# A deeper ring of split weight pieces in the expert loop of a hybrid Mamba/GLA/MoE layer

## The chip, the cores and the metric

The kernel runs on one core of one Trainium2 chip, as one program. The metric is the device time of one execution in microseconds. Three runs of the kernel before gave 2230.03, 2230.74 and 2231.86 us; the median, 2230.74 us, is the time that the changed kernel is held against.

## The reference, cut to what matters

The reference is one layer: modulation, two token mixers, and a mixture of experts of which each token takes two out of 32. The change lies in the experts. Tokens are sorted by expert into blocks of 128, and each block goes through one expert's three matrices (1024 x 512, 1024 x 512 and 512 x 1024, float32):

```python
def moe(t, w_router, router_bias, w_gate, w_up, w_down):
    ...
    def expert_block(args):
        xb, e = args
        return (jax.nn.silu(xb @ w_gate[e]) * (xb @ w_up[e])) @ w_down[e]

    yb = lax.map(expert_block, (buf.reshape(n_blocks, MOE_BLOCK, D), block_e))
    y = yb.reshape(-1, D)[dest] * gates.reshape(-1)[order][:, None].astype(t.dtype)
    return jnp.zeros_like(t).at[tok].add(y)
```

## The kernel before

The program is written engine by engine, in stages: modulation and input projection, scans, mixer and output projection, `slots` (which sorts tokens into blocks and writes a plan), `experts`, and `combine` (the final norm). Nothing reorders the instructions; each engine runs its list as written, and semaphores join the lists.

**One block.** `experts` runs a loop body once for each block; bodies come in pairs (`u` = 0 and 1, the helper `pairs`), and 50 bodies do work here. I call them even (u = 0) and odd. TensorE keeps float32 accuracy by splitting each operand into a high part of type fp32r and the rest, and making three products: high x high, low x high, high x low. A weight matrix is cut into two halves of 128 x 2048, called pieces here. The six pieces of a block are numbered by `s`. TensorE's body uses, in this order: s = 2 and 3 (w_up into `pu`), s = 4 (first half of w_gate of the next block, into `pg`), four transposes of `h` into `ph`, s = 5 (second half of that w_gate), eight transposes of the gathered tokens of the block after next into `tx`, then s = 6 and 7 (w_down into `pd`). A piece is 12 matmuls of 512 columns; each piece ends with an increment of the semaphore `used`.

**The split.** ScalarE makes the high part of a piece (`high`, L2456, a copy that rounds), VectorE the low part (`low`, L2575, raw minus high). Both write into rings, `w_hi` and `w_lo`, of three pieces each: piece s stands in slot s % 3, and `high` of piece s waits until piece s - 3 has been used. The two engines work ahead of TensorE: in a body they split s = 5 to 10, and 8 to 10 are the pieces 2 to 4 of the next body. Between the pieces they have other work. ScalarE: `h_hi` (from `ph`), `hs` = SiLU of `pg`, and `x_hi` (from `tx`, two halves). VectorE: `h` = `pu` * `hs`, `h_lo`, `x_lo` (two halves), and `yb` = `pd` * gate (two halves), which starts the block's way out. GpSimd then adds `yb` to the rows of `x_mid` by an indirect DMA, and gathers tokens by another.

**Registers.** Which expert and which of its two raw buffers a piece comes from stands in a table, the plan. Each engine loads entries of it into registers (`entry`); ScalarE loads six at the start of a body, VectorE three. The raw weights come by DMAs that SyncE issues, 2 MB for each matrix, as soon as the low part of the last piece in the other raw buffer is made.

Of the kernel before, what the change touches and what calls it, by code (L numbers as in the profile page):

```python
# [18 lines left out]
ACT = mybir.ActivationFunctionType  # L19
F32 = mybir.dt.float32  # L20
# [3 lines left out]
P = 128  # L24
# [95 lines left out]
def build(nc, A, out, debug=()):  # L120
# [16 lines left out]
    with ExitStack() as top:  # L137
# [60 lines left out]
        if "stop2" in debug:  # L198
            return
        early.close()  # L200
        route = {
            "logits": keep("logits", [P, LT, NE]), "gate": keep("gate", [P, LT, 2]),
            "bias": keep("bias", [P, NE]), "down_g": keep("down_g", [P, NG]), "down_e": keep("down_e", [P, NE]),
        }
        route["hot"] = [route["logits"], keep("hot1", [P, LT, NE])]
        mixer(nc, A, C, K, route, tok_rec, feat_rec, back_state, fwd_chunk, qk_rec, a_rows, zg_rec, w_gated, x_mid, h_rows)
# [4 lines left out]
        with ExitStack() as ctx:  # L211

            weights = [ctx.enter_context(nc.sbuf_tensor(n, [P, 2, KT * FF], F32)) for n in ("w_gates", "w_ups", "w_downs")]
            names = Names(nc, ctx, "wts")
            loaded = [names(f"{n}_loaded") for n in ("gates", "ups", "downs")]
            toks = ctx.enter_context(nc.sbuf_tensor("toks", [P, TAB, 2], I32))
            route["plan"] = ctx.enter_context(nc.sbuf_tensor("plan", [1, PL_LEN], I32))
            gate_bc = ctx.enter_context(nc.sbuf_tensor("gate_bc", [P, D], F32))
            seat(nc, ctx, "we", 96)
            w_hi = ctx.enter_context(nc.sbuf_tensor("w_hi_e", [P, 3, PIECE], mybir.dt.float32r))  # L220
            slots(nc, A, C, route, toks, weights, loaded, gate_bc, w_hi, x_mid, h_rows)
            experts(nc, A, C, route, toks, weights, loaded, gate_bc, w_hi, h_rows, x_mid)
        combine(nc, A, x_mid, out)
# [1810 lines left out]
EARLY_T = LT - 2  # L2034
PIECE = KT // 2 * FF


# [289 lines left out]

def experts(nc, A, C, route, toks, parts, w_loaded, gate_bc, w_hi, h_rows, x_mid):

    mod, ident, plan = C["mod"], C["ident"], route["plan"]
# [3 lines left out]
    with ExitStack() as ctx:  # L2342
# [14 lines left out]
        hs, h = sb("hs", [P, FF]), sb("h", [P, FF])  # L2357
        h_hi, h_lo = sb("h_hi", [P, KF, P], F32R), sb("h_lo", [P, KF, P], F32R)
        yb = sb("yb", [P, D])
        to = [sb(f"to{b}", [P, 2], I32) for b in range(2)]  # L2360
# [83 lines left out]
        SPLITS = {5: (0, 1, 1), 6: (2, 0, 0), 7: (2, 1, 0), 8: (1, 0, 1), 9: (1, 1, 1), 10: (0, 0, 2)}  # L2444

        def raw(part, half, place):
            return parts[part][:, place, PIECE * half:PIECE * (half + 1)]

        @block.scalar
        def _(act):  # L2450

            act.wait_ge(credited, 1)

            def high(s, part, half, place):

                act.activation(w_hi[:, s % 3:s % 3 + 1, :], raw(part, half, place), ACT.Copy).then_inc(hi_done, 1)  # L2456

# [8 lines left out]
            for s, part, half in ((2, 1, 0), (3, 1, 1)):  # L2466
                act.wait_ge(w_loaded[part], 16)
                if s == 3:
                    act.wait_ge(used, 1)
                high(s, part, half, slice(0, 1))  # L2470
                if s == 2:
                    features(1, 1)
# [4 lines left out]
            hold(act, w_loaded[0], order * 16 + 16, act_held)  # L2477
            high(4, 0, 0, bass.ds(par, 1))

            def body(r, u):  # L2480
                b = r * 2 + u
                pars = [entry(act, b + n, PL_PAR, 1) for n in range(3)]
                orders = [entry(act, b + n, PL_ORDER, NE - 1) for n in range(3)]

                def piece(s):
                    part, half, n = SPLITS[s]
                    if half == 0:

                        hold(act, w_loaded[part], orders[n] * 16 + 16, act_held)

# [12 lines left out]
                features(b + 2, u)  # L2503
                piece(9)
                piece(10)
# [4 lines left out]
        def _(pe):  # L2510
# [9 lines left out]

            def product(s, b, acc, a_hi, a_lo, k, at, start, stop):

                c = slice(at, at + 512)
                for n, (a, w) in enumerate(((a_hi, w_hi), (a_lo, w_hi), (a_hi, w_lo))):
                    mm = pe.matmul(acc[:, :], a[:, k, :], w[:, s % 3, c], start=start and n == 0, stop=stop and n == 2)  # L2525
                return mm

            def wide(b, s, half, u, acc):

                pe.wait_ge(lo_done, b * 6 + (s + 1 + CREDIT))  # L2530
                for k in range(4):
                    mm = product(s, b, acc, x_hi[u], x_lo[u], 4 * half + k, FF * k, half + k == 0, half == 1 and k == 3)
                mm.then_inc(used, 1)

            turn(0, 0, 0)
            pe.wait_ge(xlo_done, 2)
            wide(0, 0, 0, 0, pg)
            turn(1, 0, 1)
            wide(0, 1, 1, 0, pg)

            def body(r, u):
                b = r * 2 + u
                wide(b, 2, 0, u, pu)
                wide(b, 3, 1, u, pu)

                pe.wait_ge(xlo_done, b * 2 + 4)
                pe.wait_ge(silu_done, b + 1)
                wide(b, 4, 0, 1 - u, pg)
# [4 lines left out]
                wide(b, 5, 1, 1 - u, pg)  # L2553
                turn(b + 2, r + 1, u)
                pe.wait_ge(hlo_done, b + 1)

                pe.wait_ge(y_copied, b * 2 + 2)
                for half in range(2):
                    s = 6 + half
                    pe.wait_ge(lo_done, b * 6 + (s + 1 + CREDIT))  # L2560
                    for k in range(2):
                        for n in range(2):
                            mm = product(s, b, pd[n], h_hi, h_lo, 2 * half + k, D * k + 512 * n, half + k == 0, half + k == 2)
                    mm.then_inc(used, 1)
# [3 lines left out]
        def _(dve):  # L2568
# [3 lines left out]

            def low(s, part, half, place):

                dve.tensor_tensor(w_lo[:, s % 3:s % 3 + 1, :], raw(part, half, place), w_hi[:, s % 3:s % 3 + 1, :].bitcast(F32),  # L2575
                                  ALU.subtract).then_inc(lo_done, 1)
# [7 lines left out]
            for s, part, half in ((0, 0, 0), (1, 0, 1), (2, 1, 0), (3, 1, 1)):  # L2584
                dve.wait_ge(hi_done, s + 1)
                low(s, part, half, slice(0, 1))
                if s == 0:
# [4 lines left out]
            dve.wait_ge(hi_done, 5)  # L2592
            low(4, 0, 0, bass.ds(par, 1))

            def body(r, u):
                b = r * 2 + u
                pars = [entry(dve, b + n, PL_PAR, 1) for n in range(3)]

                def piece(s):
                    part, half, n = SPLITS[s]  # L2600
                    dve.wait_ge(hi_done, b * 6 + (s + 1))
                    low(s, part, half, bass.ds(pars[n], 1))
# [109 lines left out]
```

## Time and profile before

| what | us |
|---|---|
| median of three runs (2230.03 to 2231.86) | 2230.74 |
| the profiled execution, its own time | 2230.2 |
| its span, from the first to the last record | 2228.4 |
| busy in the span: TensorE, VectorE, ScalarE, GpSimd | 2056.6, 1662.9, 1184.4, 515.5 |

The expert loop fills about 920 us of the span, from 1237 to 2159 us; ahead of it stand the other stages, behind it a tail of 70 us that ends the last block's output and runs `combine`. A busy share is no measure of how full TensorE is, since matmuls overlap each other in the record (one is shown with 0.39 us, the next starts 0.23 us later); the distance between the starts of the same matmul in two bodies tells what a body costs. In a timeline a bracket behind a row tells how long the engine was idle ahead of it and what ended that.

### The profile page before, as it was taken

How to read it: one execution, taken by the hardware profiler on the slowest of the kernel's cores; microseconds unless marked ns; L12 is line 12 of the kernel's file. 1: busy time of each engine (PE TensorE's matmuls, PEld its weight loads, DVE VectorE, ACT ScalarE, POOL GpSimd, SP SyncE). 2: the span in 40 equal slices, each digit the busy share in tenths (PEclk: the TensorE clock that was granted, in tenths of full speed). 3: DMA queues.
4: the chain of work that ended last, by engine and by line, in shares of the span. 5: the costliest groups of instructions: out<-in, count | busy, mean ns of one | idle time of the engine just before them, and what ended most of it. 6: DMA issues, size and time to landing. Idle time of an engine off the chain costs nothing. (4 is left out here: it accounts for less than half of the span.)

```text
span 2228.4 us, 38461 instructions
## 1 busy us (share of the span) xinstructions
PE 2056.6 (92%) x12690; PEld 1701.4 (76%) x12690; DVE 1662.9 (75%) x2132; ACT 1184.4 (53%) x1564; POOL 515.5 (23%) x537
## 2 busy tenths in 40 slices
PE   5999999989999979999984999999999999999970
PEld 3998888877777768888873788888888888888850
DVE  3555555556766667777756899999999999999973
ACT  3433333434555523434332677777777777777753
POOL 1000000000100123323221233333333333333332
PEclk8999999999999969999996999999999999999995
DMA  9443344356988599999937374789888599799957
GB/s 303 157 137 126 126 142 160 109 209 203 334 293 305 209 307 338 296 325 304 302 98 266 97 242 104 234 282 304 262 282 285 168 315 365 244 356 303 376 140 311
DMA packets 219973, 541.34 MB, mean 243 GB/s; under 512 B 15968, under 2 KB 56923, under 8 KB 213339
## 3 DMA queue, kind: packets, MB, share of 16 engines
q1 hardware_dynamic: 186856, 428.68, 53.9%
q0 software_dynamic: 30512, 102.77, 17.9%
q10 hardware_dynamic: 2499, 8.45, 0.9%
q8 instruction: 69, 1.13, 0.2%
q14 instruction: 37, 0.30, 0.0%
HBM read 404.26 MB, written 135.59 MB: 242 GB/s over the span
## 5 line engine op out<-in xcount | busy, mean ns | idle before, releaser
L2456 ACT ACTIVATE w_hi_e<-w_gates 128x2048 fp32r x101 | 194.0, 1920 | 149.6 <-issue 102.7
L2575 DVE TENSOR_TENSOR w_lo_e<-w_gates,w_hi_e 128x2048 fp32r<-128x2048 f32 x103 | 236.5, 2297 | 31.2 <-ACT w_hi_e L2456 29.8
L2575 DVE TENSOR_TENSOR w_lo_e<-w_ups,w_hi_e 128x2048 fp32r<-128x2048 f32 x102 | 233.3, 2287 | 35.3 <-ACT w_hi_e L2456 35.3
L723 PE MATMUL pf<-x_hi,wide 128*128 128x256 f32 x1152 | 244.7, 289 | 11.1 <-DVE x_lo L850 11.1
L2575 DVE TENSOR_TENSOR w_lo_e<-w_downs,w_hi_e 128x2048 fp32r<-128x2048 f32 x100 | 228.1, 2281 | 0.0
L2456 ACT ACTIVATE w_hi_e<-w_ups 128x2048 fp32r (+1 forms) x102 | 195.4, 1915 | 21.7 <-PE pd_e L2525 21.7
L723 PE MATMUL pf<-x_lo,wide 128*128 128x256 f32 x720 | 204.7, 284 | 0.0
L723 PEld LDWEIGHTS pf<-x_hi,wide 128*128 128x128 f32 x1152 | 192.3, 194 | 16.2 <-issue 15.9
L2456 ACT ACTIVATE w_hi_e<-w_downs 128x2048 fp32r x100 | 191.0, 1910 | 0.5
L2525 PE MATMUL pg_e<-w_hi_e,x_hi_e 128*128 128x512 f32 x408 | 167.2, 410 | 9.6 <-DVE w_lo_e L2575 8.1
L2434 POOL DMA_INDIRECT x_mid<-yb_e,to_e x50 | 127.5, 2551 | 190.1 <-DVE yb_e L2620 188.0
L2525 PE MATMUL pd_e<-w_hi_e,h_hi_e 128*128 128x512 f32 x400 | 161.9, 405 | 0.0
L2525 PE MATMUL pg_e<-w_lo_e,x_hi_e 128*128 128x512 f32 x408 | 161.4, 396 | 0.0
L2525 PE MATMUL pg_e<-w_hi_e,x_lo_e 128*128 128x512 f32 x408 | 160.9, 394 | 0.0
L2525 PE MATMUL pu_e<-w_lo_e,x_hi_e 128*128 128x512 f32 x400 | 158.2, 395 | 0.0
L2525 PE MATMUL pu_e<-w_hi_e,x_lo_e 128*128 128x512 f32 x400 | 157.9, 395 | 0.0
L2525 PE MATMUL pd_e<-w_hi_e,h_lo_e 128*128 128x512 f32 x400 | 157.7, 394 | 0.0
L2525 PE MATMUL pu_e<-w_hi_e,x_hi_e 128*128 128x512 f32 x400 | 157.7, 394 | 0.0
L2525 PE MATMUL pd_e<-w_lo_e,h_hi_e 128*128 128x512 f32 x400 | 157.6, 394 | 0.0
L2413 POOL COPY idx_e<-toks 128x1 int32 (+1 forms) x54 | 56.7, 1050 | 417.0 <-DMA x_mid<-yb_e,to_e 338.9
L723 PEld LDWEIGHTS pf<-x_lo,wide 128*128 128x128 f32 x720 | 139.1, 193 | 0.0
L2415 POOL DMA_INDIRECT xg_e<-h_rows,idx_e x54 | 104.0, 1925 | 43.1 <-POOL idx_e L2413 42.3
(475 smaller groups left out, 4824.9 us busy)
## 6 DMA issues: line engine op xcount, KB each, us to landing
w_gates<-in_w_gate_dram SPq DMA_DIRECT2D x32, 2048.0 KB, 11.5
w_ups<-in_w_up_dram SPq DMA_DIRECT2D x32, 2048.0 KB
w_downs<-in_w_down_dram SPq DMA_DIRECT2D x32, 2048.0 KB, 10.2
recs<-tok_rec SPq DMA_DIRECT2D x17, 968.0 KB, 8.0
qk<-in_w_mod_dram SPq DMA_DIRECT2D x16, 1024.0 KB, 6.7
abc_m<-a_rows SPq DMA_DIRECT2D x16, 1024.0 KB, 7.1
qk_rec<-qk SPq DMA_DIRECT2D x14, 1024.0 KB, 3.9
qk<-qk_rec SPq DMA_DIRECT2D x14, 1024.0 KB, 8.1
```

The source lines that it names most:

```text
L723: mm = pe.matmul(pf[n % 2][:, f % 2, :], a[f][:, k, :], b[:, k, :], start=(k == 0 and j == 0), stop=(k == KT - 1 and j == 2))
L2413: pool.tensor_copy(idx[u][:, :], toks[:, bass.ds(b, 1), 0]).then_inc(idx_ready, 1)
L2415: pool.indirect_dma_start(out=xg[u][:, :], out_offset=None, in_=h_rows, in_offset=bass.IndirectOffsetOnAxis(ap=idx[u][:, 0:1], axis=0)).th ...
L2434: pool.indirect_dma_start(out=x_mid, out_offset=bass.IndirectOffsetOnAxis(ap=to[u][:, 0:1], axis=0), in_=yb[:, :], in_offset=None, compute ...
L2456: act.activation(w_hi[:, s % 3:s % 3 + 1, :], raw(part, half, place), ACT.Copy).then_inc(hi_done, 1)
L2525: mm = pe.matmul(acc[:, :], a[:, k, :], w[:, s % 3, c], start=start and n == 0, stop=stop and n == 2)
L2575: dve.tensor_tensor(w_lo[:, s % 3:s % 3 + 1, :], raw(part, half, place), w_hi[:, s % 3:s % 3 + 1, :].bitcast(F32), ALU.subtract).then_inc( ...
```

## The change

Both rings get four slots: piece s of body u stands in slot (6u + s) % 4, and `high` of piece s waits until piece s - 4 has been used. The room comes from two tiles that are dropped: `hs` now lies in the memory of the masks `incl` and `incl_bd` (joined in one tile `incls`), and `yb` in that of the router's `logits` and `hot1` (joined in `choice`); the experts read neither. In a body ScalarE now makes pieces 5, 6 and 7 ahead of `h_hi` (before: 5 and 6), and piece 8 behind it, ahead of SiLU (before: 7 there, and 8 behind SiLU). VectorE makes piece 5 ahead of `h` (before: behind it), then 6 and 7, and then `h_lo` (before: 5 and 6 between `h` and `h_lo`). Both engines load a register right ahead of the first piece that needs it, and no longer all at the body's start; the number of loads in a body stays the same. TensorE's order is unchanged.

```diff
-        C["incl"], C["incl_bd"] = keep("incl", [P, 2, P]), keep("incl_bd", [P, 2, P])
+        incls = keep("incls", [P, 2, 2, P])
...
+RING = 4
...
-        w_lo = sb("w_lo", [P, 3, PIECE], F32R)
+        w_lo = sb("w_lo", [P, RING, PIECE], F32R)
...
+        def slot(u, s):
+
+            return (6 * u + s) % RING
...
             def body(r, u):
                 b = r * 2 + u
-                pars = [entry(act, b + n, PL_PAR, 1) for n in range(3)]
-                orders = [entry(act, b + n, PL_ORDER, NE - 1) for n in range(3)]
+                pars = {}
 
                 def piece(s):
                     part, half, n = SPLITS[s]
+                    if n not in pars:
+                        pars[n] = entry(act, b + n, PL_PAR, 1)
                     if half == 0:
-
-                        hold(act, w_loaded[part], orders[n] * 16 + 16, act_held)
-
-                    hold(act, used, b * 6 + (s - 2), act_held)
-                    high(s, part, half, bass.ds(pars[n], 1))
+                        hold(act, w_loaded[part], entry(act, b + n, PL_ORDER, NE - 1) * 16 + 16, act_held)
+
+                    hold(act, used, b * 6 + (s - 3), act_held)
+                    high(u, s, part, half, bass.ds(pars[n], 1))
                 piece(5)
                 piece(6)
+                piece(7)
                 act.wait_ge(ht_ps, b + 1)
                 act.activation(h_hi[:, :, :], ph[:, :].rearrange("p (k c) -> p k c", k=KF), ACT.Copy).then_inc(hhi_done, 1)
-                piece(7)
+                piece(8)
 
                 act.wait_ge(used, b * 6 + 6)
                 act.wait_ge(h_done, b + 1)
                 act.activation(hs[:, :], pg[:, :], ACT.Silu).then_inc(silu_done, 1)
-                piece(8)
                 features(b + 2, u)
                 piece(9)
                 piece(10)
...
+                piece(5)
                 dve.wait_ge(used, b * 6 + 4)
                 dve.wait_ge(silu_done, b + 1)
                 dve.tensor_tensor(h[:, :], pu[:, :], hs[:, :], ALU.mult).then_inc(h_done, 1)
-                piece(5)
                 piece(6)
+                piece(7)
                 dve.wait_ge(hhi_done, b + 1)
                 dve.tensor_tensor(h_lo[:, :, :], ph[:, :].rearrange("p (k c) -> p k c", k=KF), h_hi[:, :, :].bitcast(F32),
                                   ALU.subtract).then_inc(hlo_done, 1)
-                piece(7)
                 piece(8)
```

How the two lists stand now. On ScalarE, from the last piece of an even body (s = 10, w_gates) into the odd body, before; a TENSOR_LOAD is a register load, of which six stand in the first gap:

```order
L2456 ACTIVATE w_hi_e<-w_gates 128x2048
L2376 TENSOR_LOAD plan
...
L2456 ACTIVATE w_hi_e<-w_gates 128x2048
...
L2456 ACTIVATE w_hi_e<-w_downs 128x2048
L2496 ACTIVATE h_hi_e<-ph_e 128x512
...
L2456 ACTIVATE w_hi_e<-w_downs 128x2048
...
L2501 ACTIVATE hs_e<-pg_e 128x512
...
L2456 ACTIVATE w_hi_e<-w_ups 128x2048
```

The same stretch of ScalarE's list after the change:

```order
L2455 ACTIVATE w_hi_e<-w_gates 128x2048
L2371 TENSOR_LOAD plan
...
L2455 ACTIVATE w_hi_e<-w_gates 128x2048
...
L2455 ACTIVATE w_hi_e<-w_downs 128x2048
...
L2455 ACTIVATE w_hi_e<-w_downs 128x2048
L2494 ACTIVATE h_hi_e<-ph_e 128x512
...
L2455 ACTIVATE w_hi_e<-w_ups 128x2048
...
L2499 ACTIVATE incls<-pg_e 128x512
```

One load stands between piece 10 and piece 5 in place of six; two moved ahead of piece 6, one ahead of piece 8 and two ahead of piece 10. Piece 7 (the second w_downs) passed `h_hi`, and piece 8 (w_ups) passed SiLU.

On VectorE, from piece 10 of the even body over `yb` into the odd body, before:

```order
L2575 TENSOR_TENSOR w_lo_e<-w_gates,w_hi_e 128x2048
L2620 SCALAR_TENSOR_TENSOR yb_e<-pd_e,to_e,gate_bc 128x512 x2
L2376 TENSOR_LOAD plan
...
L2605 TENSOR_TENSOR h_e<-pu_e,hs_e 128x512
...
L2575 TENSOR_TENSOR w_lo_e<-w_gates,w_hi_e 128x2048
...
L2575 TENSOR_TENSOR w_lo_e<-w_downs,w_hi_e 128x2048
L2609 TENSOR_TENSOR h_lo_e<-ph_e,h_hi_e 128x512
...
L2575 TENSOR_TENSOR w_lo_e<-w_downs,w_hi_e 128x2048
```

The same stretch of VectorE's list after the change:

```order
L2572 TENSOR_TENSOR w_lo_e<-w_gates,w_hi_e 128x2048
L2619 SCALAR_TENSOR_TENSOR choice<-pd_e,to_e,gate_bc 128x512 x2
L2371 TENSOR_LOAD plan
...
L2572 TENSOR_TENSOR w_lo_e<-w_gates,w_hi_e 128x2048
...
L2605 TENSOR_TENSOR h_e<-pu_e,incls 128x512
L2371 TENSOR_LOAD plan
...
L2572 TENSOR_TENSOR w_lo_e<-w_downs,w_hi_e 128x2048
...
L2572 TENSOR_TENSOR w_lo_e<-w_downs,w_hi_e 128x2048
L2609 TENSOR_TENSOR h_lo_e<-ph_e,h_hi_e 128x512
```

Piece 5 (w_gates) passed `h`, piece 7 (the second w_downs) passed `h_lo`; two pieces stand between `h` and `h_lo` as before, but they are 6 and 7.

## Rows read from the trace of the kernel before

**Rows 1.** Busy time by engine in one stretch of the expert loop, with columns
```profile
core 0: us, PE busy (x) PEld busy (x) DVE busy (x) ACT busy (x) POOL busy (x), PEclk, DMA share, GB/s
1700.00:1800.00 100.00, 99.19 (x457) 80.30 (x456) 93.25 (x67) 72.25 (x54) 35.54 (x22) 1.00 0.71 226
```
**Rows 2.** Timeline of TensorE, odd body from 1514.68, even from 1532.92: start, duration
```profile
1514.68 0.39 PE L2525 MATMUL pu_e<-w_hi_e,x_hi_e 128*128 128x512 f32 x1
...
1520.27 0.40 PE L2525 MATMUL pg_e<-w_hi_e,x_hi_e 128*128 128x512 f32 x1
...
1523.05 0.60 PE L2551 MATMUL ph_e<-ident,h_e 128*128 128x128 f32 x4
1523.57 0.50 PE L2525 MATMUL pg_e<-w_hi_e,x_hi_e 128*128 128x512 f32 x1
...
1526.47 1.03 PE L2518 MATMUL tx_e<-ident,xg_e 128*128 128x128 f32 x8
1527.26 0.48 PE L2525 MATMUL pd_e<-w_hi_e,h_hi_e 128*128 128x512 f32 x1
...
1532.92 0.39 PE L2525 MATMUL pu_e<-w_hi_e,x_hi_e 128*128 128x512 f32 x1
...
1542.15 0.50 PE L2525 MATMUL pg_e<-w_hi_e,x_hi_e 128*128 128x512 f32 x1 [0.27 <-DVE w_lo_e L2575]
...
1551.49 0.39 PE L2525 MATMUL pu_e<-w_hi_e,x_hi_e 128*128 128x512 f32 x1
```
**Rows 3.** Waits from 1100 to 2200 us: in total, times, longest
```profile
PE pg_e L2525 <- DVE w_lo_e L2575: 8.1, 26, 1.3
```
**Rows 4.** Timeline of ScalarE, the same two bodies
```profile
1518.69 1.92 ACT L2456 ACTIVATE w_hi_e<-w_gates 128x2048 fp32r x1 [1.72 <-issue]
...
1528.97 1.08 ACT L2461 ACTIVATE x_hi_e<-tx_e 128x512 fp32r<-128x512 f32 x2
1530.48 1.92 ACT L2456 ACTIVATE w_hi_e<-w_ups 128x2048 fp32r x1 [0.43 <-PE pd_e L2525]
1533.28 1.92 ACT L2456 ACTIVATE w_hi_e<-w_gates 128x2048 fp32r x1 [0.88 <-PE pd_e L2525]
1537.69 1.92 ACT L2456 ACTIVATE w_hi_e<-w_gates 128x2048 fp32r x1 [2.49 <-issue]
```
**Rows 5.** Timeline of VectorE, the same two bodies
```profile
1519.32 1.40 DVE L2620 SCALAR_TENSOR_TENSOR yb_e<-pd_e,to_e,gate_bc 128x512 f32<-128x512 f32 x2
1520.64 0.68 DVE L2605 TENSOR_TENSOR h_e<-pu_e,hs_e 128x512 f32<-128x512 f32 x1
1521.24 2.28 DVE L2575 TENSOR_TENSOR w_lo_e<-w_gates,w_hi_e 128x2048 fp32r<-128x2048 f32 x1
...
1525.64 0.68 DVE L2609 TENSOR_TENSOR h_lo_e<-ph_e,h_hi_e 128x512 fp32r<-128x512 f32 x1
...
1529.21 2.29 DVE L2575 TENSOR_TENSOR w_lo_e<-w_ups,w_hi_e 128x2048 fp32r<-128x2048 f32 x1 [0.69 <-ACT w_hi_e L2456]
1531.42 1.28 DVE L2581 TENSOR_TENSOR x_lo_e<-tx_e,x_hi_e 128x512 fp32r<-128x512 f32 x2
...
1535.34 2.29 DVE L2575 TENSOR_TENSOR w_lo_e<-w_gates,w_hi_e 128x2048 fp32r<-128x2048 f32 x1 [0.44 <-ACT w_hi_e L2456]
...
1539.77 2.33 DVE L2575 TENSOR_TENSOR w_lo_e<-w_gates,w_hi_e 128x2048 fp32r<-128x2048 f32 x1 [0.22 <-ACT w_hi_e L2456]
```
**Rows 6.** Timelines of TensorE, VectorE and SyncE at the loop's end
```profile
2158.31 0.40 PE L2525 MATMUL pd_e<-w_lo_e,h_hi_e 128*128 128x512 f32 x1
...
2163.17 1.40 DVE L2620 SCALAR_TENSOR_TENSOR yb_e<-pd_e,to_e,gate_bc 128x512 f32<-128x512 f32 x2
...
2181.92 0.84 SPq L2650 DMA_DIRECT2D x_c<-x_mid  x2
```
**Rows 7.** Timeline of ScalarE near 2104 us
```profile
2103.87 1.92 ACT L2456 ACTIVATE w_hi_e<-w_gates 128x2048 fp32r x1 [0.88 <-PE pd_e L2525]
```
**Rows 8.** The w_gates transfer issued at 2084.45 us, in the densest stretch of loads
```profile
DMA to landing us min/median/max: 16.1/16.1/16.1
```

More of the change, by code:

```diff
@@ L201, in build @@
         route = {
-            "logits": keep("logits", [P, LT, NE]), "gate": keep("gate", [P, LT, 2]),
+            "gate": keep("gate", [P, LT, 2]),
             "bias": keep("bias", [P, NE]), "down_g": keep("down_g", [P, NG]), "down_e": keep("down_e", [P, NE]),
         }
-        route["hot"] = [route["logits"], keep("hot1", [P, LT, NE])]
+        choice = keep("choice", [P, 2, LT, NE])
+        route["hot"] = [choice[:, n] for n in range(2)]
+        route["logits"] = route["hot"][0]
         mixer(nc, A, C, K, route, tok_rec, feat_rec, back_state, fwd_chunk, qk_rec, a_rows, zg_rec, w_gated, x_mid, h_rows)
@@ L2452, in _, with high @@
             act.wait_ge(credited, 1)
-            def high(s, part, half, place):
-                act.activation(w_hi[:, s % 3:s % 3 + 1, :], raw(part, half, place), ACT.Copy).then_inc(hi_done, 1)
+            def high(u, s, part, half, place):
+                n = slot(u, s)
+                act.activation(w_hi[:, n:n + 1, :], raw(part, half, place), ACT.Copy).then_inc(hi_done, 1)
             def features(b, u):
@@ L2467, in _ @@
                 act.wait_ge(w_loaded[part], 16)
-                if s == 3:
-                    act.wait_ge(used, 1)
-                high(s, part, half, slice(0, 1))
+                high(0, s, part, half, slice(0, 1))
                 if s == 2:
@@ L2519, in turn, with product, wide @@
                     mm.then_inc(xt_ps, 1)
-            def product(s, b, acc, a_hi, a_lo, k, at, start, stop):
+            def product(s, u, acc, a_hi, a_lo, k, at, start, stop):
                 c = slice(at, at + 512)
                 for n, (a, w) in enumerate(((a_hi, w_hi), (a_lo, w_hi), (a_hi, w_lo))):
-                    mm = pe.matmul(acc[:, :], a[:, k, :], w[:, s % 3, c], start=start and n == 0, stop=stop and n == 2)
+                    mm = pe.matmul(acc[:, :], a[:, k, :], w[:, slot(u, s), c], start=start and n == 0, stop=stop and n == 2)
                 return mm
-            def wide(b, s, half, u, acc):
+            def wide(b, v, s, half, u, acc):
                 pe.wait_ge(lo_done, b * 6 + (s + 1 + CREDIT))
                 for k in range(4):
-                    mm = product(s, b, acc, x_hi[u], x_lo[u], 4 * half + k, FF * k, half + k == 0, half == 1 and k == 3)
+                    mm = product(s, v, acc, x_hi[u], x_lo[u], 4 * half + k, FF * k, half + k == 0, half == 1 and k == 3)
                 mm.then_inc(used, 1)
@@ L2562, in body @@
                         for n in range(2):
-                            mm = product(s, b, pd[n], h_hi, h_lo, 2 * half + k, D * k + 512 * n, half + k == 0, half + k == 2)
+                            mm = product(s, u, pd[n], h_hi, h_lo, 2 * half + k, D * k + 512 * n, half + k == 0, half + k == 2)
                     mm.then_inc(used, 1)
@@ L2571, in _, with low @@
             dve.sem_inc(credited, 1)
-            def low(s, part, half, place):
-                dve.tensor_tensor(w_lo[:, s % 3:s % 3 + 1, :], raw(part, half, place), w_hi[:, s % 3:s % 3 + 1, :].bitcast(F32),
+            def low(u, s, part, half, place):
+                n = slot(u, s)
+                dve.tensor_tensor(w_lo[:, n:n + 1, :], raw(part, half, place), w_hi[:, n:n + 1, :].bitcast(F32),
                                   ALU.subtract).then_inc(lo_done, 1)
@@ L2585, in _ @@
                 dve.wait_ge(hi_done, s + 1)
-                low(s, part, half, slice(0, 1))
+                low(0, s, part, half, slice(0, 1))
                 if s == 0:
@@ L2592, in _ @@
             dve.wait_ge(hi_done, 5)
-            low(4, 0, 0, bass.ds(par, 1))
+            low(0, 4, 0, 0, bass.ds(par, 1))
             def body(r, u):
                 b = r * 2 + u
-                pars = [entry(dve, b + n, PL_PAR, 1) for n in range(3)]
+                pars = {}
                 def piece(s):
                     part, half, n = SPLITS[s]
+                    if n not in pars:
+                        pars[n] = entry(dve, b + n, PL_PAR, 1)
                     dve.wait_ge(hi_done, b * 6 + (s + 1))
-                    low(s, part, half, bass.ds(pars[n], 1))
+                    low(u, s, part, half, bass.ds(pars[n], 1))
+                piece(5)
                 dve.wait_ge(used, b * 6 + 4)
```

25 lines of the change are left out of this document (13 added, 12 removed).

## The prediction

> **What bounds the kernel now.** I read the busy time by stretches first. In the expert loop TensorE shows 99.19 us in 100, at a granted clock of 1.00, VectorE 93.25 and ScalarE 72.25 [rows 1]. So two engines are nearly full, and a share of busy time can't say which one sets the pace. The timeline of TensorE can: an odd body lasts from 1514.68 to 1532.92, 18.24 us, and the even one behind it to 1551.49, 18.57 us [rows 2]. In the odd body no row has a bracket: TensorE goes from product to product, and 18.24 us is what its list costs. The even body has one bracket, 0.27 us at the first product of piece 5, which waited for VectorE's low part. With the drain of the transposes ahead of it that makes 18.57 - 18.24 = 0.33 us. The group of waits has 26 such stalls and 8.1 us [rows 3]: two belong to the first body (the longest, 1.3 us, is there), and 24 are those of the even bodies 2 to 48. TensorE is the bound, and it loses 24 x 0.33 us and a start.
>
> Why is piece 5 late in even bodies alone? VectorE starts its low part 0.22 us after it could, waiting for ScalarE's high part [rows 5]. ScalarE starts that high part after 2.49 us in which it waited for nothing but its own instructions (in the odd body 1.72 us) [rows 4]: the six register loads, in the even body with the loop's branch as well. They follow high part 10, which itself waited for its slot (0.88 us, released by the last products of `pd` [rows 4]). So two things make the chain late: a ring of three, and six loads in one place. The change takes away both.
>
> The last thing I read is the end. TensorE's last product starts at 2158.31, so a next body would start 0.23 us later, at 2158.54; yet `yb` of this block starts only at 2163.17 [rows 6], 4.63 us behind. All through the loop VectorE runs that far behind TensorE: in the odd body `yb` starts at 1519.32, 4.64 us after the body's start [rows 2, 5]. Inside the loop nobody waits for `yb`; at the end everything does.
>
> **The change part by part.** It removes no work from TensorE, VectorE or ScalarE: the same pieces, the same six and three register loads. Whether TensorE still waits is worked out by laying the new lists along a body of 18.24 us, whose start is 0. From the odd body [rows 2]: piece 4 starts at 5.59, the transposes of `h` at 8.37, piece 5 at 8.89, the transposes of `tx` at 11.79, piece 6 at 12.58; piece 7, half of `pd` later, at 15.41. ScalarE starts 0.36 us after a slot is given back (1533.28 against 1532.92 [rows 2, 4]), VectorE 0.14 us after a high part ends (1533.28 + 1.92 to 1535.34 [rows 4, 5]).
>
> ScalarE first. High part 5 may start when the piece four earlier has been used, the last one of the body before: 0.36. High 6: 2.80 + 0.36 = 3.16. High 7: 5.59 + 0.36 = 5.95, done at 7.9. `h_hi` follows the transposes, 9.0 to 9.6; high 8 from 9.6 to 11.5; SiLU at 12.0; the two `x_hi` to 13.6; high 9 from there to 15.5; high 10 when piece 6 has been used, 15.41 + 0.36 = 15.77, to 17.7.
>
> VectorE: low 10 starts at 17.83 and takes 2.20 (two low parts fit in 1521.24 to 1525.64 [rows 5]), so `yb` starts at 20.03, that is 1.8 in the next body, and ends at 3.1. Low 5, whose high part has long been ready, runs to 5.3. `h` needs both pieces of `pu`: 5.59 + 0.36 = 5.95, so it ends at 6.6, and the transposes want it at 8.37: 1.7 to spare. Low 6 and low 7 run to 10.95, `h_lo` to 11.6, wanted at 12.58: 0.9 to spare. Before, `h` and `h_lo` started at the same places, 5.96 and 10.96 (1520.64 and 1525.64 less 1514.68 [rows 2, 5]), with two low parts between them, and TensorE didn't wait; so this deadline is no tighter than it was. Low 5 ends at 5.3 and is wanted at 8.89. Low 8 from 11.65, `x_lo` to 15.1, low 9 from 15.6, low 10 at 17.83: the cycle closes. Summed, VectorE has 6 x 2.20 + 1.32 + 0.60 + 0.60 + 1.28 = 17.0 us of work in 18.24, and it now idles where it waits for TensorE.
>
> The terms. (1) The 24 even bodies drop from 18.57 to 18.24: 24 x 0.33 = 8 us. Its bounds are 0 and that. (2) The tail: `yb` starts 1.8 instead of 4.63 us behind TensorE's end, 2.8 us less, once; at best it starts right behind the last product, 2158.31 + 0.40 + 0.36, which gives 4.1, and at worst nothing. What lies between `yb` and the first load of `combine` at 2181.92 [rows 6] hangs on `yb` and moves with it. (3) The first body: here the rings are still empty, both lists start late, and its stalls are shortened, but low 7 now stands ahead of `h_lo` when VectorE is behind. I take 0.6, between 0 and 1.7 (8.1 less 24 x 0.27 [rows 2, 3]). (4) The loads of registers in new places: 1.72 us idle and the 1.92 us of the high part ahead of it for six loads [rows 4] is at most 0.61 us each. One ahead of high 5 and two ahead of high 6 fit between those starts (0.36, 3.16 and the high part of 1.92). The two ahead of high 10 cost nothing if they run under high 9, and 2 x 1.72 / 6 = 0.57 us behind its end if they don't, when high 10 starts at 16.06 in place of 15.77. I take nothing, since on VectorE three loads stand between `yb` and `h`, and 1519.32 + 1.32 = 1520.64 leaves no gap [rows 2, 5]; the bound is 0.3 of term 2. The Trainium skill's page Perfetto Trace Analysis, section Sequencer Loop, says that a sequencer pushes engine instructions into a queue and executes control instructions itself; by that the loads run under the activation ahead of them. VectorE's rows agree; ScalarE's idle 1.72 us fits both readings. By that rule term 2 is 2.8, without it 2.5. (5) `hs` and `yb` at other addresses: no row shows the two at theirs and others, so I take nothing; TensorE has 1.7 us to spare behind `h`, and `yb` isn't waited for in the loop, which bounds it at some tenths either way in the tail.
>
> (6) The transfers. Every low part ends some 3 us earlier in a body (low 7 at 10.95 against 1528.52 less 1514.68 = 13.84, `h_lo` from 1525.64, then 0.60 and 2.28 [rows 5]), and the loads that wait for it start that much earlier; high 10, the first to read a new expert's w_gates, comes 18.6 - 15.8 = 2.8 us earlier (1533.28 - 1514.68 = 18.6 [rows 2, 4]). In the densest stretch a w_gates transfer takes 16.1 us [rows 8] to land, so it is there at 2100.55; the high part 10 that reads it starts at 2103.87 [rows 7], released by TensorE and not by the transfer. So 3.3 us were left, and about as many are left now. If one lands late, TensorE has low 10 in hand until 5.59 of the body after, 3.8 us later than it is made. I cost it at nothing.
>
> Sum: 2230.2 - 8.0 - 2.8 - 0.6 = 2218.8 us for the profiled execution. That one lies 0.5 us under the median of the runs, so the median should come to **2219.3 us**.
>
> **The rivals.** *A, the tail stays.* The end hangs on something other than `yb`, on GpSimd's queue or the last gather. For it: GpSimd does the output's DMA in its own order. Against it: in the timeline it waits for `yb`. Time: 2219.3 + 2.8 = 2222.1. *B, the change doesn't do what it says.* The stall only moves, to `h_lo` at piece 6 (0.9 us to spare, the least) or to a transfer in dense stretches; even bodies stay near 18.57. For it: VectorE is at 93%. Against it: the deadlines above. Time: 2230.7 less the tail, 2228 to 2231. *C, slower: `h` is now behind low 5.* Before, `h` needed no piece; now it stands in VectorE's list behind low 5, and that behind high 5. If high 5 starts where it started (4.77 in the even body: 1537.69 - 1532.92; 4.01 in the odd one: 1518.69 - 1514.68 [rows 2, 4]), low 5 runs from 6.83 to 9.03 and from 6.07 to 8.27, `h` ends at 9.7 and 8.95, and the transposes, wanted at 8.37, stall 1.4 and 0.6 us: 25 x (1.4 - 0.33 + 0.6) = 42 us, 2272 in all. It decides from the point where high 5 starts later than 8.37 - 0.68 - 2.20 - 0.14 - 1.92 = 3.4 us into a body. For it: five of the six loads only moved. Against it: none of them stands ahead of high 5 but one, and high 10 ends at 17.7, so even a whole load and the branch behind it, 0.61 + 0.77, end near 0.9.
>
> **How the numbers follow.** Forecast 0.76 (2217 to 2221.5), A 0.09, B 0.09, C 0.06. About 0.2%, 4.5 us, is what a measurement of this kernel can tell from no change, so faster means under 2226.3: the forecast and A, 0.85; the same: B, 0.09; slower: C, 0.06. The range takes in the forecast and A: from 2216, where tail and first body give all that they can, to 2224, where A has half of the even stalls left. B and C are outside.
>
> **What would show it.** Starts of the first `pu` product all 18.24 us apart from the second body on, and no bracket on `pg` from VectorE: term 1. `yb` about 1.8 us behind the body's start, in the loop and at its end: term 2. High 5 starting near 0.4, and no idle time on ScalarE that waits for nothing: term 4. A bracket at the transposes of `h` means C, one at the first `pd` product means B. I am wrong if even bodies still last 18.5 us, or if all 50 grow.

## The result and the profile after

The changed kernel takes 2210.07 us (median of four runs, 2207.72 to 2212.87), the kernel before beside it 2230.39 us (2226.56 to 2231.86): a ratio of 0.9906, 95% interval 0.9895 to 0.9918. That is 20.3 us less. The forecast was 11.4 us less, 2219.3, and the time lies below the range, which began at 2216. The direction was right, the size was not. Run again later on another occasion, the kernel took 2209.55 us, ratio 0.9905 (0.989 to 0.992).

The profiled execution took 2212.35 us, with a span of 2210.6. It answers to 2230.2 and 2228.4 of before, 17.9 us less; its expert loop started 2.9 us later (1239.63 against 1236.75 us), behind stages that the change leaves alone, and with that added back the difference is 20.7 us, within half a microsecond of that of the medians.

The same stretch of the loop as in [rows 1], busy time by engine:

```profile
core 0: us, PE busy (x) PEld busy (x) DVE busy (x) ACT busy (x) POOL busy (x), PEclk, DMA share, GB/s
1700.00:1800.00 100.00, 100.00 (x470) 82.07 (x469) 94.91 (x67) 74.93 (x57) 37.91 (x23) 1.00 0.71 223
```

TensorE's record now has no idle time at all in this stretch, and it starts 470 instructions in 100 us where it started 457: 2.8% more, although its busy time rose by 0.8% only. (The stretch is no whole number of bodies; by the body lengths below the gain in pace is 2.1%.) The timeline of TensorE, an odd body from 1511.86 and the even one from 1529.89, answers to [rows 2]:

```profile
1511.86 0.39 PE L2522 MATMUL pu_e<-w_hi_e,x_hi_e 128*128 128x512 f32 x1
...
1520.23 0.60 PE L2548 MATMUL ph_e<-ident,h_e 128*128 128x128 f32 x4
1520.58 0.48 PE L2522 MATMUL pg_e<-w_hi_e,x_hi_e 128*128 128x512 f32 x1
...
1523.44 1.03 PE L2515 MATMUL tx_e<-ident,xg_e 128*128 128x128 f32 x8
...
1529.89 0.39 PE L2522 MATMUL pu_e<-w_hi_e,x_hi_e 128*128 128x512 f32 x1
...
1547.92 0.39 PE L2522 MATMUL pu_e<-w_hi_e,x_hi_e 128*128 128x512 f32 x1
```

Both bodies last 18.03 us. Before, they lasted 18.24 and 18.57. Even bodies lost the stall that was forecast, and odd bodies, which were to be the floor, lost 0.2 us as well. The place is the four transposes of `h`: from their start to the start of piece 5 it was 1523.57 - 1523.05 = 0.52 us in the odd body before [rows 2], and is 1520.58 - 1520.23 = 0.35 us now; piece 5 behind them lasted 2.90 us up to the first transpose of `tx` and lasts 2.86. VectorE in the same odd body, answering to [rows 5]:

```profile
1513.71 1.40 DVE L2619 SCALAR_TENSOR_TENSOR choice<-pd_e,to_e,gate_bc 128x512 f32<-128x512 f32 x2
1515.03 2.28 DVE L2572 TENSOR_TENSOR w_lo_e<-w_gates,w_hi_e 128x2048 fp32r<-128x2048 f32 x1
1517.65 0.69 DVE L2605 TENSOR_TENSOR h_e<-pu_e,incls 128x512 f32<-128x512 f32 x1 [0.34 <-PE pu_e L2522]
1518.48 4.49 DVE L2572 TENSOR_TENSOR w_lo_e<-w_downs,w_hi_e 128x2048 fp32r<-128x2048 f32 x2
1522.89 0.68 DVE L2609 TENSOR_TENSOR h_lo_e<-ph_e,h_hi_e 128x512 fp32r<-128x512 f32 x1
```

Low 5 is done 3.3 us ahead of its use, `h` waits for `pu`, and `yb` starts 1.85 us into the body where it started 4.64 us in. That is not the same in every body: over the 50 it is 1.84 to 2.72 us, where it was 4.63 or 4.64 before. ScalarE, answering to [rows 4]:

```profile
1512.24 1.92 ACT L2455 ACTIVATE w_hi_e<-w_gates 128x2048 fp32r x1 [0.88 <-PE pd_e L2522]
...
1520.86 0.60 ACT L2494 ACTIVATE h_hi_e<-ph_e 128x512 fp32r<-128x512 f32 x1 [1.13 <-PE ph_e L2548]
1522.40 1.92 ACT L2455 ACTIVATE w_hi_e<-w_ups 128x2048 fp32r x1 [0.94 <-issue]
```

High 5 starts 0.38 us into the body (before: 4.0 and 4.8). The register load now stands ahead of high 8, and there ScalarE idles 0.94 us (0.40 to 1.28 us over the 50 bodies). The loop's end, timelines of TensorE, VectorE and SyncE, answering to [rows 6]:

```profile
2142.57 0.40 PE L2522 MATMUL pd_e<-w_lo_e,h_hi_e 128*128 128x512 f32 x1
...
2145.47 1.40 DVE L2619 SCALAR_TENSOR_TENSOR choice<-pd_e,to_e,gate_bc 128x512 f32<-128x512 f32 x2
...
2164.16 0.84 SPq L2649 DMA_DIRECT2D x_c<-x_mid  x2
```

`yb` starts 2145.47 - 2142.80 = 2.67 us behind TensorE's end instead of 4.63, and `combine` starts 18.69 us behind it, as before (18.75).

### The profile page after: what moved, and what is told of

Read it like the earlier page. It is cut to its first block and busy times, and to the rows that moved or that the text cites. A ratio compares the mean times of both kernels' runs of the same rounds, so it can differ in the third digit from the quotient of the medians.

```text
span 2210.6 us, 38485 instructions
## 1 busy us (share of the span) xinstructions
PE 2047.3 (93%) x12690; PEld 1702.9 (77%) x12690; DVE 1663.9 (75%) x2132; ACT 1185.3 (54%) x1564; POOL 538.0 (24%) x537
## 5 line engine op out<-in xcount | busy, mean ns | idle before, releaser
L2429 POOL DMA_INDIRECT x_mid<-choice,to_e x50 | 140.6, 2812 | 134.7 <-DVE choice L2619 132.6
```

Of the source, the lines that this page charges most:

```text
L2429: pool.indirect_dma_start(out=x_mid, out_offset=bass.IndirectOffsetOnAxis(ap=to[u][:, 0:1], axis=0), in_=yb[:, :], in_offset=None, compute ...
```

## The experiments

Two theories stood against each other for the 0.2 us that every body lost beyond the forecast. **H, a hidden wait:** in the kernel before TensorE waited for low part 5 in odd bodies too, without a bracket. **L, the layout** or something else that moved: the transposes or the operations on `hs` and `yb` became faster. A second question was which of the three edits (ring, order of the pieces on the two engines, place of the register loads) carries the gain. The table has what the traces gave; bodies are the distances between the first `pu` products, as means over 24 even and 25 odd bodies, the lag is from TensorE's end to the last `yb`.

| kernel | first body | even | odd | lag | ratio to before (95%) |
|---|---|---|---|---|---|
| before | 20.30 | 18.57 | 18.23 | 4.63 | 1 |
| changed | 19.83 | 18.03 | 18.03 | 2.67 | 0.9906 (0.9895 to 0.9918) |
| layout alone | 20.31 | 18.57 | 18.24 | 4.64 | 1.0 (0.9991 to 1.001) |
| ring alone | 20.29 | 18.19 | 18.07 | 4.09 | 0.9933 (0.9916 to 0.9949) |
| order alone (piece 5 ahead of `h`) | 21.28 | 19.57 | 18.77 | 4.64 | 1.0192 (1.0173 to 1.021) |
| loads alone | 18.74 | 18.69 | 18.51 | 5.38 | 1.0047 (1.0029 to 1.0066) |
| loads and piece 5 ahead of `h` | 18.77 | 18.64 | 18.63 | 4.63 | 1.0038 (1.0023 to 1.0053) |
| ring and piece 5 ahead of `h` | 22.84 | 18.15 | 18.10 | 4.10 | 0.9936 (0.992 to 0.9953) |
| changed, `h` first again | 18.73 | 18.50 | 18.32 | 3.33 | 0.9989 (0.9979 to 0.9998) |
| changed, loads at the start again | 22.84 | 18.03 | 18.03 | 1.84 | 0.9916 (0.9903 to 0.993) |
| changed, `yb` ahead of piece 10 | 19.83 | 18.30 | 18.09 | 0.21 | 0.9938 (0.9918 to 0.9958) |
| the same, VectorE's loads at the start | 20.98 | 18.03 | 18.03 | 0.20 | 0.9908 (0.9893 to 0.9923) |

**Layout alone.** The kernel before with `hs` and `yb` at their new addresses:

```diff
-        hs, h = sb("hs", [P, FF]), sb("h", [P, FF])
+        h = sb("h", [P, FF])
...
-        yb = sb("yb", [P, D])
...
+            hs, yb = incls[:, :, :, :].rearrange("p a b c -> p (a b c)"), choice[:, :, :, :].rearrange("p a b c -> p (a b c)")
```

> The kernel before with one thing changed: hs lies in the memory of the masks and yb in that of the router's tiles, ring of three, old orders. Theory H: nothing moves, bodies of 18.57 and 18.23 us, 2230 within 3 us. Rival L: the transposes of h or the operations on hs and yb are faster at the new addresses, both bodies lose 0.2 us, about 2220.

Measured 2232.66 against 2231.63 us: no difference, and no body moved by more than 0.04 us. L has lost its first form, the new addresses.

**`h` first again.** The changed kernel with VectorE's old order:

```diff
-                piece(5)
                 dve.wait_ge(used, b * 6 + 4)
                 dve.wait_ge(silu_done, b + 1)
                 dve.tensor_tensor(h[:, :], pu[:, :], hs[:, :], ALU.mult).then_inc(h_done, 1)
+                piece(5)
                 piece(6)
-                piece(7)
...
+                piece(7)
                 piece(8)
```

> The changed kernel with one thing put back: VectorE makes h ahead of piece 5 again (and h_lo between pieces 6 and 7). Theory H (hidden wait): in the kernel before TensorE waited for low part 5 in every body, also where the trace shows no bracket, and its own list costs 18.03 us. Then h runs from 5.95 to 6.55 us of a body, low 5 ends at 8.83, TensorE wants it at 8.72, so each body lasts 18.2 to 18.25 us, the transposes of h are followed by piece 5 after about 0.52 us and not 0.35, and the time is 49 x 0.2 = 10 us above the changed kernel, about 2220. Rival L (layout): the 0.2 us came from the new addresses of hs and yb or from something else that is kept here; then bodies stay at 18.03 us and the time at 2210.

Measured 2229.06 against 2231.63 us. H expected 2220, L 2210. Bodies went back to 18.32 and 18.50 us with all else kept, so L's second form falls too, and the order on VectorE is needed, as H says; but they overshot what H expected. VectorE and TensorE show both the wait and the overshoot; VectorE first, then TensorE:

```profile
1501.15 0.69 DVE L2604 TENSOR_TENSOR h_e<-pu_e,incls 128x512 f32<-128x512 f32 x1 [1.12 <-PE pu_e L2522]
1502.09 2.29 DVE L2572 TENSOR_TENSOR w_lo_e<-w_gates,w_hi_e 128x2048 fp32r<-128x2048 f32 x1 [0.25 <-issue]
...
1520.42 2.29 DVE L2572 TENSOR_TENSOR w_lo_e<-w_gates,w_hi_e 128x2048 fp32r<-128x2048 f32 x1 [0.17 <-issue]
```
```profile
1504.44 0.51 PE L2522 MATMUL pg_e<-w_hi_e,x_hi_e 128*128 128x512 f32 x1 [0.19 <-DVE w_lo_e L2572]
...
1522.77 0.50 PE L2522 MATMUL pg_e<-w_hi_e,x_hi_e 128*128 128x512 f32 x1
```

Piece 5 starts at 1504.44, 0.06 us behind low 5's end (1502.09 + 2.29 = 1504.38), and in the odd body at 1522.77, again 0.06 us behind it (1522.71). One of the two has a bracket and the other has none; both wait. That is the sign, and the rows of before had it already: in the even body 1542.15 against 1539.77 + 2.33 = 1542.10, in the odd one 1523.57 against 1521.24 + 2.28 = 1523.52 [rows 2, 5], 0.05 us in each. The overshoot is the register load that now stands between `h` and low 5: 0.25 and 0.17 us in which VectorE waits for nothing but its own list. Without these the bodies would last about 18.25 and 18.15 us (an estimate: 18.50 and 18.32 less the two), so the old order by itself costs 0.1 to 0.2 us a body here and the load the rest.

The wait does have a bracket in the kernel before, on other rows. The profile lists TensorE's weight loads (PEld) apart from its products. In the odd body of [rows 2] the one that follows the four of the transposes waited for low 5:

```profile
1522.82 0.59 PEld L2551 LDWEIGHTS ph_e<-ident,h_e 128*128 128x128 f32 x4
1523.57 0.19 PEld L2525 LDWEIGHTS pg_e<-w_hi_e,x_hi_e 128*128 128x128 f32 x1 [0.16 <-DVE w_lo_e L2575]
```

In the view of waits from 1100 to 2200 us that [rows 3] is taken from, the weight loads have a row of their own. It counts one stall at piece 5 in each of the 50 bodies and one more in the first. Before, and then the changed kernel, where only that one more is left:

```profile
PEld pg_e L2525 <- DVE w_lo_e L2575: 18.6, 51, 1.5
```
```profile
PEld pg_e L2522 <- DVE w_lo_e L2572: 0.9, 1, 0.9
```

**Ring alone.** The kernel before with four slots and the room for them:

```diff
-                    hold(act, used, b * 6 + (s - 2), act_held)
+                    hold(act, used, b * 6 + (s - 3), act_held)
```

> The kernel before with the ring of four (and the layout that makes room for it), register loads all at the body's start and old orders. Theory H: high 10 starts 2 us earlier or more, six loads behind it take 3.6 to 4.4 us from its start, so high 5 starts 1 to 2 us into a body and not 4 to 4.8; low 5 then follows h directly, 5.95 + 0.60 + 2.28 = 8.83, and TensorE wants it at 8.72: all bodies 18.2 to 18.25 us, the bracket of the even bodies gone, 24 x 0.33 = 8 us and about 1 us of tail, about 2221. If the ring alone made the whole gain: 18.03 us, 2210. If the loads made the even body late and not the ring: 18.57 and 18.23, 2230.

Measured 2218.04 against 2231.63 us, ratio 0.9933: two thirds of the gain. The bodies are shorter than expected, 18.07 and 18.19 us (the even ones 18.16 without the last, which lasted 18.91 because a high part waited 1.8 us for its w_gates transfer). VectorE lags less, 4.1 us instead of 4.6, so `h` starts as soon as `pu` is there, 5.85 us into the even body shown where it started 5.96 us in, and low 5 with it. The wait is nearly gone, not wholly; VectorE, then TensorE:

```profile
1500.62 0.69 DVE L2606 TENSOR_TENSOR h_e<-pu_e,incls 128x512 f32<-128x512 f32 x1 [0.35 <-PE pu_e L2526]
1501.23 2.28 DVE L2576 TENSOR_TENSOR w_lo_e<-w_gates,w_hi_e 128x2048 fp32r<-128x2048 f32 x1
```
```profile
1503.13 0.60 PE L2552 MATMUL ph_e<-ident,h_e 128*128 128x128 f32 x4
1503.57 0.50 PE L2526 MATMUL pg_e<-w_hi_e,x_hi_e 128*128 128x512 f32 x1
```

Piece 5 still starts 0.06 us behind low 5's end (1503.51), here 0.44 us behind the transposes and not 0.35, without a bracket; in the odd bodies it is 0.36 us. The Trainium skill, page Perfetto Trace Analysis, section Optimization Strategy, says that a gap repeated on the engine that should be full can mean too few buffers; this run agrees: the ring alone took away the brackets of the even bodies, but for the one with the late transfer.

**Ring and piece 5 ahead of `h`**, without the other moves:

```diff
+                piece(5)
                 dve.wait_ge(used, b * 6 + 4)
                 dve.wait_ge(silu_done, b + 1)
                 dve.tensor_tensor(h[:, :], pu[:, :], hs[:, :], ALU.mult).then_inc(h_done, 1)
-                piece(5)
```

> Ring of four, register loads all at the body's start, and on VectorE piece 5 ahead of h; all else as before (piece 7 behind h_lo, 8 behind SiLU on ScalarE). Theory H: high 5 starts 1 to 2 us into a body, low 5 ends ahead of h, h ends at 7.4 or earlier and is wanted at 8.37: all bodies 18.03 us; yb starts 3 to 4 us behind a body's start, so the time is 1 to 2 us above the changed kernel, 2211 to 2212. If the spread loads are needed: bodies above 18.1 us and 2215 or more.

Measured 2218.88 us, not 2211: no better than the ring alone. The first body costs 22.84 us, and the others 18.10 and 18.15. Here high 7 still stands behind `h_hi`. VectorE waits for it, and `yb` still starts 4.1 us into the next body, with low 5 and then `h` behind it; VectorE, then TensorE:

```profile
1504.52 0.69 DVE L2607 TENSOR_TENSOR h_e<-pu_e,incls 128x512 f32<-128x512 f32 x1
...
1508.50 2.29 DVE L2576 TENSOR_TENSOR w_lo_e<-w_downs,w_hi_e 128x2048 fp32r<-128x2048 f32 x1 [0.49 <-ACT w_hi_e L2459]
1511.29 2.29 DVE L2576 TENSOR_TENSOR w_lo_e<-w_ups,w_hi_e 128x2048 fp32r<-128x2048 f32 x1 [0.50 <-ACT w_hi_e L2459]
```
```profile
1505.26 0.65 PE L2552 MATMUL ph_e<-ident,h_e 128*128 128x128 f32 x4
1505.67 0.48 PE L2526 MATMUL pg_e<-w_hi_e,x_hi_e 128*128 128x512 f32 x1
```

The transposes start 0.05 us behind the end of `h` (1505.21): again a wait without a bracket on the products, at another place. It hardly delays their start; the loss is behind it, where piece 5 follows after 0.41 us and not 0.35. So pieces 7 and 8 had to move too: the run with the loads at the start, further down, differs from this one by their places alone, and its bodies last 18.03 us.

**Order alone**, the same edit on the kernel before, with three slots:

> The kernel before with one thing changed: VectorE makes piece 5 ahead of h. Ring of three, loads at the body's start. This sets the price of rival C of the prediction: h stands behind a piece whose high part starts 4.0 us (odd) or 4.77 us (even) into a body. Theory H (TensorE's list costs 18.03 us): h ends at 9.0 and 9.7, the transposes want it at 8.37, bodies of 18.65 and 19.4 us, 25 x 1.25 = 31 us more, about 2262. With a list of 18.24 us, as the prediction took it: 18.85 and 19.6 us, about 2272. If the order alone made the gain: 2220 or less.

Measured 2272.66 against 2231.11 us. This is rival C: 2272 was named for it. By theory H it should have been 2262; the bodies are 18.77 and 19.57 us, not 18.65 and 19.4. The transposes wait for `h` in every body, start 0.06 us behind its end, and piece 5 follows them after 0.41 us and not 0.35, neither of which H had in its sum. The waits show the place, in total, times and longest:

```profile
PE ph_e L2551 <- DVE h_e L2606: 46.4, 50, 2.3
```

**Loads alone**, each register ahead of its first piece, in the kernel before:

```diff
-                pars = [entry(act, b + n, PL_PAR, 1) for n in range(3)]
-                orders = [entry(act, b + n, PL_ORDER, NE - 1) for n in range(3)]
+                pars = {}
```

> The kernel before with one thing changed: each register is loaded ahead of the first piece that needs it, on ScalarE and VectorE. Ring of three, old orders. Theory H: high 10 still starts at 18.6 us and ends 2.3 us into the next body, high 5 then waits for its slot, 2.80 + 0.36 = 3.2 us, and ends at 5.1, ahead of h; low 5 follows h and ends at 8.83, wanted at 8.72: all bodies 18.2 to 18.25 us, bracket of the even bodies gone, yb still 4.6 us behind, about 2222. If only a deeper ring cures the even bodies: 18.57 and 18.23, 2230.

Measured 2239.95 against 2231.11 us: slower, where both views expected faster or nothing. High 5 did start as worked out, 3.2 us into the body, but the loads stood in the way elsewhere. ScalarE, VectorE, and two groups of waits:

```profile
1530.60 0.60 ACT L2502 ACTIVATE hs_e<-pg_e 128x512 f32<-128x512 f32 x1 [0.66 <-PE pg_e L2526]
1532.41 1.91 ACT L2456 ACTIVATE w_hi_e<-w_ups 128x2048 fp32r x1 [1.22 <-issue]
```
```profile
1534.46 2.30 DVE L2576 TENSOR_TENSOR w_lo_e<-w_ups,w_hi_e 128x2048 fp32r<-128x2048 f32 x1 [2.01 <-ACT w_hi_e L2456]
```
```profile
ACT w_hi_e L2456 <- issue: 28.8, 47, 1.3
...
PE pu_e L2526 <- DVE w_lo_e L2576: 4.0, 12, 0.4
```

One load between SiLU and high 8 lets ScalarE idle for 1.22 us here, VectorE waits 2.01 us for that piece (0.69 before [rows 5]), and TensorE waits at a place where it never waited. And VectorE's load between `h` and low 5, up to 0.20 us, keeps piece 5 late: it still starts 0.05 us behind low 5's end in every body but the first.

**Loads and piece 5 ahead of `h`**, three slots: the two edits above together.

> The kernel before with two things changed: spread register loads, and on VectorE piece 5 ahead of h; ring of three. It asks what the fourth slot is worth beside the two others. Theory H: low 10 ends 4.6 us into a body, yb at 5.9, low 5 at 8.1, h at 8.8, wanted at 8.37: all bodies about 18.5 us, about 2235, slower than before although the loads are spread. If the ring is not needed: 18.03 us, 2212.

Measured 2239.39 against 2231.11 us, bodies of 18.63 us (expected 18.5, and about 2235). The ring is needed: without it `h` is late in every body (waits, in total, times and longest):

```profile
PE ph_e L2552 <- DVE h_e L2609: 18.1, 49, 0.5
```

**Changed, loads at the start again:**

```diff
-                pars = {}
+                pars = [entry(act, b + n, PL_PAR, 1) for n in range(3)]
+                orders = [entry(act, b + n, PL_ORDER, NE - 1) for n in range(3)]
```

> The changed kernel with one thing put back: all register loads at the body's start, on ScalarE and VectorE. Ring of four and new orders stay. Theory R (the spread loads are no part of the gain; a load that stands between two operations whose waits are over costs 0.2 us or more): high 5 starts 1.1 to 1.9 us into a body instead of 0.4, which nobody feels, since low 5 is made from 3 us on; VectorE loses the 0.1 to 0.3 us gap between h and piece 6; bodies 18.03 us, 2210 within 2 us of the changed kernel. If the spread loads carry part of the gain: bodies of 18.1 us or more, 2214 and up.

Measured 2212.16 us, beside 2209.55 for the changed kernel on the same chip; both against 2230.23. From the second body on all last 18.03 us, to the hundredth. The waits say it best:

```profile
ACT w_hi_e L2455 <- issue: 102.5, 49, 2.5
PE ph_e L2547 <- DVE h_e L2602: 2.3, 1, 2.3
```

ScalarE idles 102.5 us behind its register loads, 49 times, as much as before the change, and TensorE does not feel it after the first body. There, six loads behind the loop's entry make high 5, low 5 and with it `h` late, rival C in one body: 2.3 us, and 22.84 us instead of 19.83. In the traces the spread loads are worth these 3 us, once, and cost 0.8 us at the end (lag 2.67 against 1.84); the two medians lie 2.6 us apart, with ranges that overlap.

**The changed kernel again**, as the measure for that run and the next:

> The changed kernel once more, as the measure for the two beside it: bodies of 18.03 us, 2210 within 3 us.

Measured 2209.55 us, bodies of 18.03 us.

**Changed, `yb` ahead of piece 10**, to take the rest of the tail:

```diff
-                piece(10)
                 dve.wait_ge(used, b * 6 + 8)
...
+                piece(10)
```

> The changed kernel with one thing more: on VectorE yb stands ahead of piece 10. Inside the loop nothing waits: yb from 0.4 us of the next body to 1.7, low 10 to 3.9 (wanted at 5.59), low 5 to 6.1, h to 6.8 (wanted at 8.37), h_lo to 11.8 (wanted at 12.4): bodies stay at 18.03 us. At the loop's end yb starts 0.4 us behind TensorE's last product and not 2.67: 2.2 us less, about 2208. If the output's end hangs on something else than yb: 2210. If h or h_lo comes late: bodies of 18.1 us or more, 2214 and up.

Measured 2217.7 against 2231.11 us, not 2208. The lag is gone (0.21 us), but bodies grew to 18.30 and 18.09. VectorE and two groups of waits:

```profile
1501.53 0.69 DVE L2605 TENSOR_TENSOR h_e<-pu_e,incls 128x512 f32<-128x512 f32 x1
1503.15 4.49 DVE L2572 TENSOR_TENSOR w_lo_e<-w_downs,w_hi_e 128x2048 fp32r<-128x2048 f32 x2 [0.94 <-issue]
```
```profile
DVE w_lo_e L2572 <- issue: 21.6, 39, 1.0
...
PE pd_e L2522 <- DVE h_lo_e L2609: 3.0, 10, 0.8
```

A register load between `h` and piece 6 now lets VectorE idle for 0.94 us here and 1.0 at most, and `h_lo` comes late: the deadline with the least to spare in the prediction, 0.9 us.

**The same with VectorE's loads at the body's start:**

```diff
-                pars = {}
+                pars = [entry(dve, b + n, PL_PAR, 1) for n in range(3)]
```

> The changed kernel with yb ahead of piece 10 on VectorE, and VectorE's register loads at the body's start, where they run under piece 10. Theory R: the bodies of 18.3 and 18.09 us of the version with yb first came from the register load between h and piece 6 (0.65 and 0.94 us idle there), which made h_lo late; with the loads at the start the bodies are 18.03 us again, and the end gains 1 to 2 us over the changed kernel, 2208 to 2209. If the early yb itself made h_lo late: bodies above 18.05 us with a bracket at the first pd product, 2214 or more.

Measured 2210.41 us, beside 2209.55 for the changed kernel: the same. The bodies are 18.03 us again, so it was the load and not the early `yb`. What the tail gains, the start loses: `yb` starts 2.5 us earlier behind TensorE's end, but the first load of `combine` follows it after 20.1 us instead of 18.8, and the first body costs 1.15 us more. The 1.3 us lie in GpSimd's issue of the last output, which starts 2.2 us behind `yb` in both and takes 2.86 us here against 1.60; why, no run shows. No version that was run beats the changed kernel.

## Why the prediction was wrong

**The step that failed is the floor.** "In the odd body no row has a bracket: TensorE goes from product to product, and 18.24 us is what its list costs." It costs 18.03. Term 1 was capped by that ("its bounds are 0 and that"), and so the range could not hold the time. By the traces: even bodies 24 x (18.57 - 18.03) = 13 us instead of 8, odd bodies 25 x (18.23 - 18.03) = 5 us instead of none. Together 18.1 where 8.0 was forecast. What the runs showed in place of the floor is a wait: in every body of the kernel before, the odd ones too, piece 5 started 0.05 us behind low 5's end.

| term | forecast | measured in the traces |
|---|---|---|
| 1, even bodies | 8.0 | 13.1 |
| odd bodies | 0 | 5.1 |
| 2, tail | 2.8 | 1.96 |
| 3, first body | 0.6 | 0.47 |
| sum | 11.4 | 20.6 |

The sum agrees with the 20.3 us between the medians. Term 3 was taken, not worked out, and that it came near is luck, though both effects named for it are there: a wait of 1.26 us at piece 5 went, and one of 0.82 us at the first `pd` product, for `h_lo`, came. Two slips changed nothing: the upper bound of term 3 is 8.1 - 24 x 0.27 = 1.6 and not 1.7, and A with half of the even stalls left is 2226, not 2224.

**What the rows said, unread.** A bracket is idle time in a record where ends of products are modelled and overlap the next start. The four transposes are shown with 0.60 us, and their next product can follow after 0.35; a wait of up to about 0.2 us fits under that and leaves no bracket on the products. Three signs stood in the trace. The weight loads had the bracket, 51 times, in the same view as the 26 stalls of [rows 3]. Piece 5 started 0.05 us behind the end of low 5 in both bodies. And the odd body gave four transposes 0.52 us when eight of `tx` took 0.79 (1526.47 to 1527.26 [rows 2]). The Trainium skill, page Perfetto Trace Analysis, section Identifying the Most-Contended Engine, warns that matmul busy time does not tell how close TensorE is to its limit, since pipelined instructions look smaller in the trace. The traces agree with the warning, not with its direction: 99.19 us busy in 100 made TensorE look full while it lost 2.1% of its pace.

**Why piece 5 was late, half right.** I named two causes, a ring of three and six loads in one place, and wrote that the change takes away both. The runs separate them. The ring is the larger part, alone 13.3 us of the loop's 18.6 (921.8 to 908.5 us; the changed kernel 903.2). With the ring and the new orders the loads cost a body nothing: put back, they leave every body from the second on at 18.03 us. Without the ring they do make high 5 late, 4.0 and 4.8 us into a body against 3.2 when they are spread, but spreading them made the kernel slower. What I missed is a third cause, the order on VectorE: low 5 stood behind `h`, and `h` behind `pu`. The new orders of pieces 5, 7 and 8 give the rest of the gain. Of these, piece 5 ahead of `h` was run without the ring, where it costs 42 us; 7 and 8 were not run by themselves.

**The lists laid along a body held** where no register load mattered: high 5 at 0.36 (measured 0.38), high 6 and 7 released by TensorE, `h` waiting for `pu` and not for a piece. `h_lo` kept its place well enough not to stall from the second body on, and no transfer made a piece late: the profile puts 19 of ScalarE's waits down to one, but the pieces behind them start where they start in the other bodies. In the last body `yb` started 2.67 us behind instead of 1.8.

**Term 4, the register loads, was too cheap.** I took nothing for them and bounded a load by 0.61 us. The one ahead of high 8 was not priced at all: ScalarE idles 0.94 us there in the body shown and 1.24 in the last, high 8 starts 10.5 and 10.8 us into them and not 9.6, and the tail is 0.8 us longer. With the loads of both engines at the start, high 8 starts at 9.5 in every body from the second on and the lag is 1.84, the 1.8 of the forecast. The rows of VectorE on which I rested the zero had their loads between `yb` and `h`; between `h` and the next piece a load left up to 0.26 us idle in the changed kernel and 1.0 with `yb` first. Why the place matters was not tried.

**The rivals.** A and B did not come. C came in an experiment: with piece 5 ahead of `h` and high 5 where it started before, the time was 2272.66 against the 2272 named for it. That close an agreement is part luck: the loop grew by 38.3 us (921.8 to 960.1) where C gave 42 on the wrong floor, and the loop started 2.6 us later in that trace. It did not come in the changed kernel, because high 5 starts at 0.38 us, far ahead of the 3.4 us from which C decides.

**Left open.** Why a single register load holds ScalarE for anything from 0.4 to 1.3 us was not tried. Nor was the drift of about 3 us in the stages ahead of the loop, which is in kernels that do not differ there.

## What to carry to other kernels

Before calling a period the floor of an engine, compare the start of every instruction that has a producer with that producer's end: here a constant 0.05 us was a wait, with or without a bracket on the products. Read the waits of the weight loads beside those of the products. The same group of instructions costing more per piece in one place than in another is another sign. Give a ring its extra slot before reordering, and move the producers of the tightest deadline only with that slot: the same move was part of the gain with it and cost 42 us without. Put register loads where their idle time has slack behind it, as at the start of a body here, and not right behind an operation that others wait for; that too is what these runs show, not a rule.

## What the runs showed of the hardware

With six register loads in a row ScalarE's next high part started 3.64 us behind the start of the one ahead of them, 0.61 us a load [rows 4]. The Trainium skill, page DMA: Bandwidth & Descriptors, section Latency and other measured facts, gives about 0.6 us as the least for one, and the row agrees. A single one cost less regularly: 0.40 to 1.28 us of idle time ahead of high 8 in the changed kernel, 1.22 us in the row of the version with the loads alone, and on VectorE between nothing and 1.0 us. And the addresses of `hs` and `yb`, for which I had no row, do not matter: ratio 1.0 (0.9991 to 1.001).
